# Two blocks of attention logits issued earlier, in banks of their own, in a two-layer encoder kernel on one core

## What is computed

```python
for i in range(DEPTH):                       # 2 layers, SEQ 256, D_MODEL 1024
    h = _rmsnorm(x, pre_norm_g[i])
    z = h @ w_in[i]
    qa, ka, va, qi, ki, wi, ga, qb, kb, vb, gb = _split_in(z)
    # ... rotary on the first 16 of 64 elements of every q and k head
    oa = _dsa_attention(qa, ka, va, qi, ki, wi, top_k)     # group A: 8 heads, the 64 best keys of an indexer
    ob = _diff_attention(qb, kb, vb, lam, lam_init, subln_g[i])   # group B: 4 heads of softmax1 - lam * softmax2
    y = jnp.concatenate([oa * silu(ga), ob * silu(gb)], axis=-1) @ w_out[i]
    x = x + _rmsnorm(y, post_norm_g[i])
    gate = jax.nn.sigmoid(x @ w_ple_gate[i])
    x = x + _rmsnorm((p[i] @ w_ple_proj[i]) * gate, ple_norm_g[i])
```

## Time and profile before

| | |
|---|---|
| median of 3 runs | 364.26 us (364.06 to 365.84) |
| profiled execution, its own time | 365.38 us |
| its span, first to last instruction | 363.6 us |
| TensorE (PE) busy | 352.9 us, 97%, 1905 matmuls |
| VectorE (DVE) busy | 265.2 us, 73% |
| ScalarE (ACT) busy | 227.0 us, 62% |
| GpSimd (POOL) busy | 72.2 us, 20% |
| mean granted TensorE clock | 0.996 |
| DMA | 61.12 MB, 168 GB/s on average |

### The profile page before, as it was taken

The page is one execution under the profiler, slowest core; times in us unless marked ns, Lnnn a source line. Parts: engine busy times, 40 slices in busy tenths (PEclk is TensorE's granted clock), DMA queues, the critical chain, the costliest instruction groups (busy, mean ns, idle before and its releaser), DMA issues.

```text
span 363.6 us, 5649 instructions
## 1 busy us (share of the span) xinstructions
PE 352.9 (97%) x1905; PEld 291.1 (80%) x1905; DVE 265.2 (73%) x557; ACT 227.0 (62%) x455; POOL 72.2 (20%) x121
## 2 busy tenths in 40 slices
PE   6999999999999999999999999999999999999992
PEld 5897787788888888888888878878888788888881
DVE  2786678889966586786786578878996658678543
ACT  4794566785767863664674656778576786365221
POOL 1153455042500000003015514004250000000000
PEclk9999999999999999999999999999999999999998
DMA  7994468764573465548665845447458336550011
GB/s 261 379 349 115 117 178 113 289 219 123 165 237 121 123 225 173 174 154 150 213 194 162 251 139 167 130 118 206 123 162 249 131 115 233 167 164 18 2 55 61
DMA packets 31948, 61.12 MB, mean 168 GB/s; under 512 B 2376, under 2 KB 4688, under 8 KB 31920
## 3 DMA queue, kind: packets, MB, share of 16 engines
q1 hardware_dynamic: 30784, 57.48, 50.2%
q0 software_dynamic: 1120, 3.28, 4.6%
q10 hardware_dynamic: 16, 0.00, 0.0%
HBM read 59.71 MB, written 1.05 MB: 167 GB/s over the span
## 4 chain that ended last, share of the span: by engine, by line
PE 92%; issue 3%; POOL 2%; ACT 1%; DVE 1%; DVEq 0%; POOLq 0%
PE proj L1083 25%; PE proj L1085 24%; PE proj L1084 24%; PE sc L1199 3%; PE sc L1140 3%; PE tr L1212 2%; PE tr L1156 2%; PE pv L1233 2%; PE pv L1228 1%; PE proj L1033 1%; PE proj L1029 1%; PE proj L1042 1%; PE sc L1170 1%; POOL v_all L502 1%; PE sc L1049 1%
## 5 line engine op out<-in xcount | busy, mean ns | idle before, releaser
L1083 PE MATMUL proj<-w_hi,act_hi 128*128 128x512 f32 (+1 forms) x400 | 161.0, 402 | 0.0
L1085 PE MATMUL proj<-w_hi,act_lo 128*128 128x512 f32 (+1 forms) x400 | 155.3, 388 | 0.0
L1084 PE MATMUL proj<-w_lo,act_hi 128*128 128x512 f32 (+1 forms) x400 | 154.9, 387 | 0.0
L766 DVE TENSOR_TENSOR w_lo<-raw,w_hi 128x1024 fp32r<-128x1024 f32 (+1 forms) x102 | 122.5, 1213 | 19.0 <-ACT w_hi L569 18.2
L569 ACT ACTIVATE w_hi<-raw 128x1024 fp32r<-128x1024 f32 (+1 forms) x102 | 103.5, 1034 | 2.9 <-PE proj L1085 1.5
L1085 PEld LDWEIGHTS proj<-w_hi,act_lo 128*128 128x128 f32 x400 | 75.1, 188 | 15.9
L1083 PEld LDWEIGHTS proj<-w_hi,act_hi 128*128 128x128 f32 x400 | 75.2, 188 | 15.5 <-issue 0.7
L1084 PEld LDWEIGHTS proj<-w_lo,act_hi 128*128 128x128 f32 x400 | 75.3, 188 | 13.0
L512 POOL TENSOR_TENSOR rstd<-var,minus_half 128x1 f32<-128x1 f32 x12 | 6.7, 555 | 182.1 <-DVE var L756 168.2
L680 ACT ACTIVATE probs<-probs,neg_max 128x128 f32<-128x128 f32 (+1 forms) x64 | 28.2, 445 | 1.9 <-DVE neg_max L903 1.9
L569 ACT ACTIVATE act_hi<-sc 128x512 fp32r<-128x512 f32 x20 | 11.2, 598 | 19.6 <-PE sc L1140 19.6
(11 more groups left out here) (162 smaller groups left out, 425.2 us busy)
## 6 DMA issues: line engine op xcount, KB each, us to landing
raw<-in_w_in_dram SPq DMA_DIRECT2D x59, 512.0 KB, 3.8
raw<-in_w_out_dram SPq DMA_DIRECT2D x16, 512.0 KB, 3.4
raw<-in_w_ple_gate_dram SPq DMA_DIRECT2D x16, 512.0 KB, 3.5
raw<-in_w_in_dram SPq DMA_DIRECT2D x7, 324.0 KB, 6.3
raw<-in_w_ple_proj_dram SPq DMA_DIRECT2D x4, 512.0 KB, 3.6
resid<-in_x_dram SPq DMA_DIRECT2D x2, 512.0 KB, 7.3
probs<-in_w_in_dram SPq DMA_DIRECT2D x2, 512.0 KB, 9.6
g_ple<-in_ple_norm_g_dram POOLq DMA_DIRECT2D x2, 512.0 KB, 7.0
```

The source lines that it names most:

```text
L766: nc.vector.tensor_tensor(w_lo[:, g % SLOTS, 0:nk * cols], landing(g, nk * cols), w_hi[:, g % SLOTS, 0:nk * cols].bitcast(fp32), ALU.subtr ...
L1083: nc.tensor.matmul(ps, src_hi[:, b, k0 + k, :], hi, start=(first_u and k == 0), stop=False)
L1084: nc.tensor.matmul(ps, src_hi[:, b, k0 + k, :], lo, start=False, stop=False)
L1085: last = nc.tensor.matmul(ps, src_lo[:, b, k0 + k, :], hi, start=False, stop=last_k)
```

## The change

The logits of S 2 are issued on TensorE right behind those of S 1, and those of S 5 right behind S 4, into proj[2] (even task) and pv (odd task) instead of sc[0] and sc[1]. On ACT and DVE the steps keep their places. So that proj[2] is free, the chunks KB to GA use three banks 0, 1, 3 in turn, with new counts to wait for. PT 0 moves from place 19 to 18, PV 3 from 43 to 45. PV 0 and PV 3 get a wait for DVE's reading of pv (max_done 6 and 12 of the layer). S 1 waits for max_done 2, S 3 for 4 (before: 6), S 4 for 8.

```diff
+S_AHEAD = {1: 2, 4: 5}
...
-    PT=[19, 23, 26, 41, 42, 44, 45, 50, 51],
-    PV=[20, 25, 28, 43, 50, 52],
+    PT=[18, 23, 26, 41, 42, 44, 45, 50, 51],
+    PV=[20, 25, 28, 45, 50, 52],
...
-            return 2 * (IN_CHUNKS.index(chunk) % 2) + b
+            if chunk in ("IDX", "QB"):
+                return 2 * IN_CHUNKS.index(chunk) + b
+            return [0, 1, 3][(2 * (IN_CHUNKS.index(chunk) - 2) + b) % 3]
...
+        def s_bank(i):
+
+            return [proj[2], pv][i % 2] if i // 2 in S_AHEAD.values() else sc[i % 2]
...
-                                out=probs[:, i % 4, j * keys:(j + 1) * keys], in0=sc[i % 2][:, j * keys:(j + 1) * keys],
+                                out=probs[:, i % 4, j * keys:(j + 1) * keys], in0=s_bank(i)[:, j * keys:(j + 1) * keys],
...
                 elif chunk == "VB":
-                    pe.wait_ge(z_out, L * 8 + b + 1)
+                    pe.wait_ge(z_out, L * 8 + 2 + b)
                 elif chunk == "QA":
-                    pe.wait_ge(z_out, L * 8 + 2 + b + 1)
+                    pe.wait_ge(*((z_out, L * 8 + 4) if b == 0 else (v_out, L * 4 + 1)))
                 elif chunk == "KA":
-                    pe.wait_ge(v_out, L * 4 + b + 1)
+                    pe.wait_ge(*((v_out, L * 4 + 2) if b == 0 else (z_out, L * 8 + 5)))
                 elif chunk == "VA":
-                    pe.wait_ge(z_out, L * 8 + 4 + b + 1)
+                    pe.wait_ge(z_out, L * 8 + 6 + b)
                 elif chunk == "GB":
-                    pe.wait_ge(z_out, L * 8 + 6 + b + 1)
+                    pe.wait_ge(*((z_out, L * 8 + 8) if b == 0 else (v_out, L * 4 + 3)))
                 elif chunk == "GA":
-                    pe.wait_ge(v_out, L * 4 + 2 + b + 1)
+                    pe.wait_ge(*((v_out, L * 4 + 4) if b == 0 else (glu_done, L * 4 + 1)))
...
+            def logits(L, n, g, b, keys):
+
+                for j in range(N // keys):
+                    for part in range(1 if b == 0 else 3):
+                        for odd in range(2):
+                            m = s_task(2 * n + odd)[2][j]
+                            rows = slice(odd * HEAD, (odd + 1) * HEAD)
...
+                            ins = nc.tensor.matmul(s_bank(2 * n + odd)[:, j * keys:(j + 1) * keys], q, k,
+                                                   start=(part == 0), stop=end)
+                            if end and j == N // keys - 1:
+                                ins.then_inc(s_done, 1)
...
+                elif kind == "S" and s[1] in S_AHEAD.values():
+                    continue
                 elif kind == "S":
...
-                        pe.wait_ge(max_done, L * 12 + 2 * s[1])
...
+                        pe.wait_ge(max_done, L * 12 + {1: 2, 3: 4, 4: 8}[s[1]])
+                    logits(L, s[1], g, b, keys)
+                    if s[1] in S_AHEAD:
+                        if s[1] == 1:
+                            pe.wait_ge(z_out, L * 8 + 1)
+                        else:
+                            pe.wait_ge(pv_out, L * 4 + 2)
+                        logits(L, S_AHEAD[s[1]], g, b, keys)
...
+                    if m in (0, 3):
+                        pe.wait_ge(max_done, L * 12 + (6 if m == 0 else 12))
```

More of the change, by code:

```diff
@@ L1012, in wait_bank @@
                     pe.wait_ge(wo_scaled, L * 4 + 2 * b + n + 1)
+            def logits(L, n, g, b, keys):
[4 more added lines that the diff above has]
+                            rows = slice(odd * HEAD, (odd + 1) * HEAD)
+                            if b == 0:
+                                q, k = qT[g][rows, m // 2, 0:P], kT[rows, m // 2, :]
+                            else:
+                                q = (q_lo if part == 2 else q_hi)[rows, m // 2, :]
+                                k = (k_lo if part == 1 else k_hi)[rows, m // 2, :]
+                            end = part == (0 if b == 0 else 2)
+                            ins = nc.tensor.matmul(s_bank(2 * n + odd)[:, j * keys:(j + 1) * keys], q, k,
+                                                   start=(part == 0), stop=end)
+                            if end and j == N // keys - 1:
+                                ins.then_inc(s_done, 1)
             def wait_tr(L, s):
@@ L1174, in _ @@
                                 ins.then_inc(dots_done, 1)
+                elif kind == "S" and s[1] in S_AHEAD.values():
+                    continue
                 elif kind == "S":
                     g, b, _, keys = s_task(2 * s[1])
-                    n_maps = N // keys
                     keys_from = ("KB" if g == 0 else "KA", b)
```

## The result

The changed kernel takes 367.44 us as the median of 16 runs (365.71 to 368.17), against 365.58 for the kernel before in 16 runs (364.0 to 366.87). The ratio is 1.0054, with a 95% interval of 1.0040 to 1.0067. On 365.6 us that ratio makes 1.97 us more, between 1.5 and 2.4; the two medians lie 1.86 apart. The forecast was 1.36 us more and 365.6 us in all. The median of before, on which it was set, had come from three runs and was 1.3 us lower than that of the 16.

What follows compares the result with a forecast made beforehand. TensorE was taken as the bound, without slack. Per layer -0.40 - 0.26 + 0.83 + 0.28 + 0.05 (PT 5 late) + 0.18 = +0.68, for two layers +1.36: 364.26 + 1.36 = 365.6 us, 8-in-10 range 363.9 to 367.0.

Steps and rivals of the forecast that it cites:

- What bounds the kernel: TensorE, busy 352.9 of 363.6 us, has no slack: list length saved and every new wait reach the span.
- The list gets shorter by 0.66 per layer: TensorE's list saves 0.40 us at tasks four and five and 0.26 at tasks ten and eleven.
- The second place: Tasks ten and eleven (S 5, PV 3 from 43 to 45): 2.57 us becomes 2.31, saving 0.26 per layer.
- PT 0's wait: PT 0 at place 18 waits for DVE's combination (mix_done) from 69.21 to 70.04: 0.83 us lost per layer.
- rival B: The waits do not come about and only the shorter list remains: 362.9 us, chance 0.12.
- PV 0 covered: DVE's reading of tasks four and five ends by 72.8, PV 0 comes at 73.2: covered by 0.4 us, no cost.
- The bank's wait: With three banks, GB's first unit for rows 128 to 255 waits for VA's copy on ACT: 0.28 us per layer.
- Rival C: Only VA's eviction and PT 5 are in time, because ACT gains a little: 364.7 us, chance 0.08.
- the base: The forecast change of 1.36 us was set on the median of 364.26 us, giving 365.6.
- the restarts: After each of three TensorE waits, weights not loaded ahead cost 0.06 us, 0.18 per layer.
- Rival A: Slower: each of three waits costs a full 0.27 us restart instead of 0.06, giving 366.9 us; chance 0.17.
- rival D: TensorE's clock falls, so the unit behind each large wait runs at 1.2 GHz: 368.3 us, chance 0.03.

Runs made afterwards that it cites:

- The second profile: The kernel before, unchanged, profiled again: first KB unit at 35.28 us against 36.19, KB to output projection 100.51 and 100.22 us in both.
- the first experiment: The changed kernel with PT 0 back at place 19 instead of 18: ratio to the kernel before 1.0033 (1.0021 to 1.0046).

## Why the prediction was right or wrong

**What bounds the kernel: right.** In every run what TensorE's list lost or won in a layer came through whole. Where the runs with intervals can be set against the ruler, twice the change per layer lies inside them.

**The list gets shorter by 0.66 per layer: right, a little low.** With no wait left the layer is 0.72 us shorter in layer 1, and 0.75 in layer 0, of which 0.03 stand ahead of every change. The second place gives the 0.26 that was forecast (-0.46 ahead of GB, -0.72 behind it, in layer 1). The first gives 0.46 instead of 0.40. The second half of the logits costs 0.71 (63.93 to 65.55 for 24 against 0.91 for 12), as taken; what is missing are hundredths in the units behind the blocks, which the sum had not counted. The Trainium skill ("TensorEngine Tiling (Array Packing)", Tiling Modes) says that a change of tiling mode drains TensorE. The trace agrees as far as it goes: the block of 24, in one mode, runs on in its middle at 0.12 per pair, and what the change saves was at the entries and exits. No run here shows that a drain is what they consist of.

**PT 0's wait: right in place and cause.** The release stood still against the layer's start, at 69.99 in the kernel before and 70.58 here with a start-up 0.60 later. Moving PT 0 and PV 0 off it gave back the loss. So rival B, that the waits would not come about, is refuted. **PV 0 covered: right** in the changed kernel (it follows its unit by 1.36 there, 72.58 to 73.94). **The bank's wait: right**, one boundary of six, 0.29 forecast as 0.28, and shown by itself in two runs. Rival C, which had ACT in time, is refuted with it.

**The first failed step is the base**, "set on the median, the forecast is 364.26 + 1.36 = 365.6". The kernel before measures 365.58 in 16 runs, 1.3 us more. Of the 1.84 us between the forecast and the measured 367.44 this is by far the most: on 365.58 the same sum of +1.36 gives 366.9. The three runs behind 364.26 took 365.84, 364.26 and 364.06; among the 16, which hold them, six lie at 364.0 to 364.4 and nine at 365.3 to 366.9, so two of the three were low ones by bad luck. The profiled execution had taken 365.38; the prediction noted that this was 1.1 above the median and kept to the median. The second profile shows one source of such spread, 0.9 us of start-up, ahead of every step that the change moves.

**The second failed step is the restarts**, "Between nothing and 0.10 I take 0.06 for each of three waits, 0.18", with the release of 0.05 us for all three. The mechanism was right and this term of the sum mis-sized: 0.37 per layer instead of 0.18, so 0.38 us in all. What each wait cost beyond 0.05 after its releaser is about 0.12 at PT 0 (0.10 of it in the release, the rest in its next unit), 0.13 at GB's unit (its second step, 0.34 instead of 0.23, and a little behind it), and 0.12 at PT 5. With 0.37 my sum gives -0.40 - 0.26 + 0.83 + 0.28 + 0.05 + 0.37 = +0.87, against 0.84 and 0.85. I had taken one release and used it for all; PT 0 and PT 5 start 0.15 and 0.14 behind theirs. Why is open. It is not that they are transposes, since PT 6 started 0.05 behind ACT's copy in the run with PT 5 at 45. Rival A had the right mechanism, with 0.27 per wait where about 0.12 was measured.

**The chances.** 1.0054 is just past the bound of 0.5%, with an interval on both sides of it. I gave 0.22 to slower, of which 0.15 was rival A. Of the 1.97 us, 1.69 are shown by the traces between KB and the output projection. The remaining 0.28 is inside the interval of the ratio. The start-up, 0.60 later in this profile than in the first of the kernel before, could hold it, but that is not shown.

**The clock (rival D).** It did not fall at the waits. The mean granted clock is 0.995, against 0.996 before, and behind PT 0 the steps from 71.11 on are 0.32, 0.22 and 0.23. The reason that was given beforehand is weaker than it looked, though: the earlier trace rows give 1.00 for 4 to 8 us, and in that very stretch the transposes of the kernel before took twice as long as in its second profile.

## What to carry to other kernels

When one engine has no slack, joining two blocks of it saves what entering and leaving a block costs, but every step that this brings forward must be checked against the moment of its releaser, and every buffer that is given away against the queue of the engine that empties it. Here 0.72 us per layer was there to be had, and three waits of 0.96, 0.42 and 0.17 ate more than that; moving nine entries of the table of places by one each won it back. Take the base from as many runs as the result: here three runs had it 1.3 us too low, as much as the whole change that was forecast. Moving a step on one engine moves its counterpart on the others: ask what that one will then stand behind. And short waits of a pipelined engine are in no table of waits: lay the starts of equal steps in both traces side by side.

## What was not expected of the hardware

- Work held by a semaphore starts 0.05 to 0.26 us behind the end of its releaser: GB's unit 0.05 and PT 6 0.05, both behind a copy of ACT, PT 5 0.14, PT 0 0.15, PV 0 in the first experiment 0.26. So the kind of the held work does not decide it; what does is open. Behind the projection matmul the next step is 0.34 instead of 0.23.
- A change of PSUM banks within a run of paired 64-row matmuls costs nothing that can be seen (0.12 us per pair on both sides of it).
- The first microseconds of TensorE run at half pace for a time that differs between executions (four transposes in 0.91 or 0.49 us), under a granted clock that reads 1.00 either way.
- The stretch of 100 us between two points of a layer repeats within 0.01 us in the two profiles of one kernel, while the start-up moves by 0.9. Here one profile told a change of 0.10 to 0.14 us in a layer (PT 2 at 27) whose intervals from twelve timed runs overlap.
